# Two transformer blocks on one core: the first product behind each norm takes x times the gain, and 1/rms is applied to what leaves PSUM

## The reference, cut to what matters

```python
def first_block(x, mem, ...):
    for l in range(DEPTH):                                                     # DEPTH = 2
        x = x + FFN_RES_WEIGHT * swiglu_ffn(rms_norm(x, ffn1_norm_g[l]), ...)    # n = 0
        proj = rms_norm(x, mix_norm_g[l]) @ w_mix_in[l]                         # n = 1
        ...                                                # RWKV time mix, local attention
        x = x + jnp.concatenate([y_rwkv, y_moba], axis=-1) @ w_mix_out[l]
        x = x + memory_cross_attention(rms_norm(x, xattn_norm_g[l]), ...)       # n = 2
        x = x + FFN_RES_WEIGHT * swiglu_ffn(rms_norm(x, ffn2_norm_g[l]), ...)    # n = 3
    return rms_norm(x, final_norm_g)
```

## Time and profile before

| | us |
|---|---|
| median of 3 runs (lowest to highest) | 2770.87 (2770.12 to 2775.54) |
| the profiled execution's own time | 2772.01 |
| its span in the trace | 2770.0 |
| PE busy in the span | 2631.0 |
| DVE busy | 1680.3 |
| ACT busy | 1020.7 |
| mean granted TensorE clock | 0.973 of full speed |

### The profile page before, as it was taken

The page is one execution under the profiler, slowest core; times in us unless marked ns, Lnnn a source line. Parts: engine busy times, 40 slices in busy tenths (PEclk is TensorE's granted clock), DMA queues, the critical chain, the costliest instruction groups (busy, mean ns, idle before and its releaser), DMA issues. The chain is left out here.

```text
span 2770.0 us, 44598 instructions
## 1 busy us (share of the span) xinstructions
PE 2631.0 (95%) x18787; PEld 2325.1 (84%) x18787; DVE 1680.3 (61%) x2235; ACT 1020.7 (37%) x1241; POOL 99.2 (4%) x179
## 2 busy tenths in 40 slices
PE   8999989889999999989979999999999999989999
PEld 8999888879989999888879974355699899737999
DVE  6877655657777777656648742364455555354555
ACT  4335303434333345204443322453333333254333
POOL 2110000000100100000001100000000000000000
PEclk9999989999999999999999999999999999999999
DMA  8776201535767775003527772100355555210452
GB/s 274 258 258 195 80 1 47 190 130 184 259 229 233 259 241 168 31 1 109 196 91 235 260 259 77 61 16 16 122 183 182 196 184 183 93 61 31 137 183 92
DMA packets 279509, 415.62 MB, mean 150 GB/s; under 512 B 10105, under 2 KB 235721, under 8 KB 277698
## 3 DMA queue, kind: packets, MB, share of 16 engines
q1 hardware_dynamic: 260332, 348.16, 38.1%
q0 software_dynamic: 18128, 64.20, 6.6%
q10 hardware_dynamic: 902, 1.15, 0.1%
HBM read 399.82 MB, written 13.65 MB: 149 GB/s over the span
## 5 line engine op out<-in xcount | busy, mean ns | idle before, releaser
L572 PE MATMUL ps<-h_high,w_high 128*128 128x256 f32 x2112 | 609.1, 288 | 27.5 <-DVE h_low L1305 15.0
L574 PE MATMUL ps<-h_high,w_low 128*128 128x256 f32 x2144 | 613.0, 286 | 0.0
L572 PEld LDWEIGHTS ps<-h_high,w_high 128*128 128x128 f32 x2112 | 412.7, 195 | 32.8 <-issue 29.3
L574 PEld LDWEIGHTS ps<-h_high,w_low 128*128 128x128 f32 x2144 | 418.3, 195 | 0.0
L573 PE MATMUL ps<-h_low,w_high 128*128 128x256 f32 x1408 | 401.4, 285 | 0.0
L1320 DVE TENSOR_TENSOR w_low<-ring,w_high 128x2048 fp32r<-128x2048 f32 x132 | 301.9, 2289 | 132.7 <-ACT w_high L1080 132.6
L2659 DVE TENSOR_TENSOR w_low<-ring,w_high 128x2048 fp32r<-128x2048 f32 x96 | 220.0, 2292 | 240.7 <-ACT w_high L2443 240.5
L1080 ACT ACTIVATE w_high<-ring 128x2048 fp32r<-128x2048 f32 x132 | 251.6, 1914 | 267.8 <-DMA ring<-in_ffn_w_in 150.6
L2443 ACT ACTIVATE w_high<-ring 128x2048 fp32r<-128x2048 f32 x96 | 183.8, 1916 | 331.4 <-PE ps L2122 304.3
L573 PEld LDWEIGHTS ps<-h_low,w_high 128*128 128x128 f32 x1408 | 273.6, 194 | 0.0
L1341 DVE SCALAR_TENSOR_TENSOR mod_acc<-wmod,cond,mod_acc 128x512 f32<-128x512 f32 x336 | 230.5, 746 | 0.0
(11 more groups left out here) (411 smaller groups left out, 5168.1 us busy)
## 6 DMA issues: line engine op xcount, KB each, us to landing
ring<-in_w_mlp SPq DMA_DIRECT2D x96, 1024.0 KB, 5.4
ring<-in_ffn_w_in SPq DMA_DIRECT2D x88, 1024.0 KB, 8.3
wmod<-in_w_mod POOLq DMA_DIRECT2D x96, 512.0 KB, 6.3
ring<-in_ffn_w_out SPq DMA_DIRECT2D x44, 1024.0 KB, 5.1
ring<-in_w_mix_in SPq DMA_DIRECT2D x26, 1024.0 KB, 5.5
ring<-in_xattn_w_kv SPq DMA_DIRECT2D x16, 1024.0 KB, 5.4
mod_scratch<-mod_acc POOLq DMA_DIRECT2D x24, 512.0 KB, 5.4
ring<-mod_scratch SPq DMA_DIRECT2D x12, 1024.0 KB, 6.9
```

Source lines behind the costliest of these rows:

```text
L572: mm(dst, w_hi, x_hi, start=start, stop=False, **more)
L574: return mm(dst, w_lo, x_hi, start=False, stop=stop, **more)
```

## The change

For the seven norms other than the very first, ACT writes `high` straight from x times the gain as soon as a pair of x is final (`gained_high`), and DVE the rest (`gained_low`). The first product behind the norm runs on these, without 1/rms; what leaves PSUM is multiplied by 1/rms (`by_root`), now by DVE: in the FFN the first gate and up products (before and beside the SiLU), in the mix its first tile, in the cross attention all four `xq` tiles (which ACT evacuated before). For n = 2 the normed operand is no longer made at all; for the others it is made as before and the second product waits for it. The sums move between the pairs of the first product. On ACT the squares of norm 3 move ahead of the weight tiles, and two table preloads go. The copies of `mem` move ahead of layer 0's mix norm on DVE.

```diff
 # PE
+        def gained_pair(l, n, p):
+            pe.wait_ge(*g_low_ready.at(*gained_at(l, n, 2 * p + 1)))
...
             def first_gate_up():
                 halves = [parts(r, 0, r, r) for r in range(2)]
+                if f:
+                    pe.wait_ge(*x_ready.at(l, 4 * 2 + 3))
                 for p in range(KD // 2):
-                    pe.wait_ge(*h_ready.at(l, H_READY[3 * f] + SPLIT_AT[p]))
-                    for r, bank in ((0, 4), (1, 6)):
+                    for q in (((), (3,), (), ()) if f else ((), (1, 2), (3,), ()))[p]:
+                        sums(l, 3 * f, q)
+                    gained_pair(l, 3 * f, p)
+                    for r, bank in ((0, 5), (1, 6)):
...
-                for q in range(1, 4):
-                    if then:
-                        sums(*then, q)
...
-            gate_up(1, 1, 2, 2, False)
+            gate_up(1, 1, 2, 2, False, normed(l, 3 * f) if l or f else None)
...
+                if n == 0:
+                    def first_pair(p):
+                        for q in ((), (1, 2), (3,), ())[p]:
+                            sums(l, 1, q)
+                        gained_pair(l, 1, p)
+                    column_tile(l, ("mix_in", j), mix_bank(0), g_high, g_low, before=first_pair)
...
-            sums(l, 2, 3)
+            def xq_pair(p):
+                if p == 2:
+                    sums(l, 2, 3)
+                gained_pair(l, 2, p)
             for j in range(LIN_TILES):
-                column_tile(l, ("xq", j), 4 + j % 4, h_high, late_low, before=None if j else normed(l, 2))
+                column_tile(l, ("xq", j), xq_bank(j), h_high, late_low, before=None if j else xq_pair)
...
 # ACT
+        def gained_high(l, n, q):
+
+            high, _ = gained(n)
+            for k in (2 * q, 2 * q + 1):
+                go(high[:, k, :], x_sb[:, k, :], ACT.Copy, scale=gain_of(l, n, k)).then_inc(*g_high_ready.up())
...
-            if n == 3:
-                col_high(l, XO0 + 3, XO0 + 1)
-            if n == 3 or (n == 0 and l):
-                first_high(l, n // 3)
+            if n == 0 and l:
+                first_high(l, 0)
...
-            nc.scalar.preload_act_table_set(LN_EXP)
+            if n < 2:
+                nc.scalar.preload_act_table_set(LN_EXP)
...
+                if n or l:
+                    gained_high(l, n, q)
+                if n == 2 and q == 2:
+                    col_high(l, XQ0 + 1)
+                if n == 3 and q == 0:
+                    w_high_part(FfnTiles(l, 1), 0, 0, 0, 0)
+                    col_high(l, XO0 + 3, XO0 + 1)
+                if n == 3 and q == 1:
+                    w_high_part(FfnTiles(l, 1), 1, 0, 0, 1)
...
 # DVE
+        def gained_low(l, n, q):
+
+            high, low = gained(n)
+            for k in (2 * q, 2 * q + 1):
+                dve.wait_ge(*g_high_ready.at(*gained_at(l, n, k)))
+                v.scalar_tensor_tensor(low[:, k, :], x_sb[:, k, :], gain_of(l, n, k), high[:, k, :],
+                                       ALU.mult, ALU.subtract).then_inc(*g_low_ready.up())
...
             w_low_of(0, 1, 2, 2)
-            times_up(0, 0, 0, False)
+            if l or f:
+                dve.wait_ge(*std_ready.at(l, 6 * f + 2))
+                for r, dst, bank in ((0, prob, 5), (1, act_whole, 6)):
+                    dve.wait_ge(*tiles.used(r, 0, 0))
+                    v.tensor_tensor(dst[:, 0, :].rearrange("p (m t) -> p m t", m=2),
+                                    ps[bank].rearrange("p (m t) -> p m t", m=2), by_root(), ALU.mult
+                                    ).then_inc(*first_scaled.up())
...
-            dve.wait_ge(*mix_evac.at(l, n + 1))
             b = raw[:, n % 2]
+            if n:
+                dve.wait_ge(*mix_evac.at(l, n))
+            else:
+                dve.wait_ge(*column_used(l, MIX_ORDER[0]))
+                dve.wait_ge(*std_ready.at(l, 4))
+                step(l, v.memset(raw[:, :, :, 0:1], 0.0), mixed)
+                step(l, v.tensor_tensor(b[:, :, 1:T + 1], ps[mix_bank(0)].rearrange("p (m t) -> p m t", m=2),
+                                        by_root(), ALU.mult), raw_evac)
...
-            norm(l, 2, "xattn_norm_g")
+            col_low(l, XQ0 + 1)
             col_low(l, XQ0 + 2)
-            modulate(l, 0, second, range(0, 4))
+            dve.wait_ge(*std_ready.at(l, 6))
+            modulate(l, 0, second, range(0, 2))
+            xq_scaled(l, 0)
+            modulate(l, 0, second, range(2, 4))
+            xq_scaled(l, 1)
             col_low(l, XQ0 + 3)
             col_low(l, XO0)
+            xq_scaled(l, 2)
             modulate(l, 0, second, range(4, 6))
             col_low(l, XO0 + 1)
+            xq_scaled(l, 3)
             softmax(l, XH, NH, XD ** -0.5, (T, T), cross_out(l))
```

More of the change, by code:

```diff
@@ L300, in build_first @@
         late_low = part("late_low", [P, KD, T])
+        part("under_mem", [P, KD, T])
+        part("under_hank", [P, NH, T])
+        g_low = part("g_low", [P, KD, T])
+        part("under_low", [P, RAW + 4 * T - KD * T])
+        g_high = part("g_high", [P, KD, T])
         w_high.append(h_low[:, :, :].rearrange("p k t -> p (k t)"))
@@ L612, in first_gate_up, with gate_up @@
                             last.then_inc(w_used[tiles.slot(r, 0)].sem, 1)
-            def gate_up(i, b, t, buffer, reuse):
-                for r, bank in ((0, 4 + b), (1, 6 + b)):
+            def gate_up(i, b, t, buffer, reuse, before=None):
+                for r, bank in ((0, 5 - b), (1, 6 + b)):
                     hi, lo = parts(r, b, t + r, (buffer + r) % W_HIGHS)
@@ L621, in gate_up @@
                         for k in range(KD):
+                            if before and r == 0 and m == 0 and k % 2 == 0:
+                                before(k // 2)
                             cols = slice(m * P, (m + 1) * P)
@@ L1286, in residual, with first_low, one_behind, after @@
                     after(q)
[L1288 to L1289 removed]
+        def first_low(l, f, rs=(0, 1)):
+            for r in rs:
                 w_low_part(FfnTiles(l, f), r, 0, r, r)
+        def gained_low(l, n, q):
[4 more added lines that the diff above has]
+                                       ALU.mult, ALU.subtract).then_inc(*g_low_ready.up())
+        def one_behind(l, n):
+            def after(q):
+                for p in ((), (0,), (1,), (2, 3))[q]:
+                    gained_low(l, n, p)
+            return after
         def col_low(l, c):
@@ L1396, in ffn @@
                 col_low(l, 1)
-            residual(l, 3 * f, [None] * 3 + [tiles.n0 + FFN_TILES - 1], 0.5)
+            residual(l, 3 * f, [None] * 3 + [tiles.n0 + FFN_TILES - 1], 0.5,
+                     None if f and l + 1 == DEPTH else one_behind(l + f, 1 - f))
         def step(l, instruction, signal=None):
@@ L1555, in recurrence, with mix_out_after, xq_scaled, xo_after @@
                                         ALU.mult), seq_step)
+        def mix_out_after(l, q):
+            if q < 3:
+                col_low(l, MIX_OUT0 + 2 + q)
+            gained_low(l, 2, q)
+        def xq_scaled(l, j):
+            n = FIRST_AT[("xq", j)]
+            dve.wait_ge(w_used[n % RING].sem, freed(n, l) + 1)
+            v.tensor_tensor(xq[:, 2 * j:2 * j + 2, :], ps[xq_bank(j)].rearrange("p (m t) -> p m t", m=2),
+                            by_root(), ALU.mult).then_inc(*xq_evac.up())
+        def xo_after(l, q):
+            gained_low(l, 3, q)
+            if q == 0:
+                first_low(l, 1, (0,))
+                col_low(l, XO0 + 3)
+            if q == 1:
+                first_low(l, 1, (1,))
         w_low_part(FfnTiles(0, 0), 0, 0, 0, 0)
@@ L1580, in vector_program @@
                 v.tensor_copy(bias_rows, ps[1][0:NH, :]).then_inc(*mem_placed.up())
-            step(l, v.memset(raw_buf[:, :], 0.0), mixed)
+            norm(l, 1, "mix_norm_g")
             for n, j in enumerate(MIX_ORDER[:7]):
@@ L1674, in vector_program @@
             modulate(l, 0, second, range(6, KD))
-            residual(l, 2, [FIRST_AT[("xo", j)] for j in range(LIN_TILES)], 1.0,
-                     lambda q: col_low(l, XO0 + 3) if q == 1 else first_low(l, 1) if q == 2 else None)
+            residual(l, 2, [FIRST_AT[("xo", j)] for j in range(LIN_TILES)], 1.0, lambda q: xo_after(l, q))
             norm(l, 3, "ffn2_norm_g")
```

133 lines of the change are left out of this document (84 added, 49 removed).

## The result

| | before | after |
|---|---|---|
| median of the runs taken together | 2773.2 us (4 runs) | 2742.25 us (2741.4 to 2746.6, 4 runs) |
| profiled execution: time, span | 2772.01, 2770.0 | 2742.86, 2740.9 |
| mean granted clock | 0.973 | 0.973 |

After over before is 0.9892, with a 95% interval of [0.9875, 0.9909]: about 1.1% faster, by 31.0 us between the medians and 25 to 35 us by the interval. The forecast was 2728 with a range up to 2741, and the median lies 1.25 us outside it. The gain forecast was 42.6.

The account below looks back on a forecast made before the run. PE was taken as the bound, busy 95%, with about 47 of 139 idle us at the seven norms. Terms 14.6 + 13.9 + 7.4 + 6.3 + 3.4 - 2.4 - 0.6 = 42.6 us gave a 2728.3 us median, range 2717 to 2741.

Parts of the forecast that it names:

- The second block and the FFN steps past the second are the same.: Claim that the second block and FFN steps beyond the second keep their time; no gain or loss counted there.
- half rate after the short new waits: Rival: new waits of 0.6 to 2.1 us halve the clock, 1.9 us at six places, 11.4; 2740 us, chance 0.15.
- only the 6.1 us wait pays: Reading of the skill page: clock falls only behind the wait at step 1's gate tile, layer 1's FFN 1; 1.9 us.
- FFN 2, layers 0, 1: Norm 3 and FFN 2: earlier squares and first products on the gained operand; 14.6 and 13.9 us gained.
- `xq`, layers 0, 1: Norm 2 and xq product: it starts right after the sums, so cross attention comes 7.4 and 6.3 us earlier.
- mix, layers 1, 0: Norm 1 and the mix's first tiles: 3.4 us gained in layer 1, 0.6 us lost in layer 0.
- norm 0 of layer 1: Layer 1's first FFN: step 0 starts earlier, but step 1's gate tile waits 6.1 us; 2.4 us lost.
- the walk: Each engine's operation list timed part by part from unit prices; 38 to 47 us gained, chance 0.53, forecast 2728.
- The prices: Assumed unit times: gain multiplication 0.49 us, `gained_low` 0.4 to 0.48, multiplying a bank by 1/rms 0.69.
- At nothing: ACT's gain multiplications (3.9 us a norm) and DVE's `gained_low` (3.4) lie hidden under PE's work, costing nothing.
- The slower rival: Rival: without norm gaps the weight DMA falls behind in three FFNs; at 1.5 us a step, 2778 us, chance 0.03.
- the signs named beforehand: Trace signs: right, about 2 us before cross attention; wrong, mix clock at 0.50 or waits at step 1's up tile.

Follow-up runs that it names:

- e9: Kernel before, one added DVE reduction lengthening PE's wait at the entry of the second block's first attention; 2790.99 us, ratio 1.0062.
- e10: Changed kernel, extra matmuls filling only the third wait, at the entry of the second block's attention, in both layers; 2731.83 us, ratio 0.9855.
- e11: Changed kernel unaltered, timed again in one job; 2732.89, 2733.31, 2743.57 and 2744.32 us.
- e1: Changed kernel, extra matmuls filling PE's three last waits before the second block's attention, in both layers; 2731.54 us, ratio 0.9844.
- e4: Changed kernel, 16 extra matmuls ahead of the second block's first product; 2751.12 us, one run.
- e7: Changed kernel, 4 extra matmuls ahead of the second block's first product, same program as e2, timed in rounds; 2735.93 to 2751.48 us, median 2747.24.
- e3: Changed kernel, 8 extra matmuls ahead of the second block's first product; 2736.88 us, one run.
- e5: Kernel before with only ACT's order at norm 3 changed (first squares ahead of weight halves, no table preload there); 2756.63 us, ratio 0.9952.
- e8: Kernel before with extra matmuls filling the three waits before the second block's attention; 2772.27 us, ratio 1.0001.
- e2: Changed kernel, 4 extra matmuls ahead of the second block's first product; 2726.17 us, one run.
- e6: Changed kernel with the three waits filled as in e1 and step 1's weight halves made ahead of the norm; 2716.82 us, ratio 0.9810.

## Why the prediction was wrong

**The step that failed** is "The second block and the FFN steps past the second are the same." Its instructions and waits are; its clock is not. In the two profiled executions the second block, from the first key rotation to the first output product, went from 117.9 to 137.3 us: 19.4 lost, after 4.6 gained ahead of it (6.3 us of clock lost there before, 1.6 after). With 42.8 at its start and 1.1 behind it that makes the 29.1 of the spans. e9 and e10 show the cause from both sides. I had priced a fall of the clock by the matmuls that follow it in the first block, where I took 1.9 to 3 us each; none of my cases had one that lasts. The trace of before had them all the same: in layer 0's time mix, among products of 64 and 128 columns, its windows from 384 to 396 are at 0.50, one of them (388 to 392) with PE busy 4.00 of 4.00. Where the changed kernel is spared, it ran at 2732.9 and 2733.3 (e11), inside the range, though 5 us above the forecast of 2728.

**The rival "half rate after the short new waits"** gave 2740, near the median, and that is luck. Its mechanism is there at two of its places. In the changed kernel's own trace the clock falls 1 us behind layer 1's wait of 1.84 us (1408.59), for 3.4 us:

```profile
1408.00:1410.00 2.00, 1.41 (x10) 0.90 1.08 369
1410.00:1412.00 2.00, 2.00 (x11) 0.50 0.91 280
1412.00:1414.00 2.00, 2.00 (x15) 0.75 0.64 224
```

All eight traces with the changed first block (after, e1 to e4, e7, e10, e11) have this fall, and three of them (e1, e3, e11) one like it behind layer 0's wait at 618 to 620; in the changed kernel's trace the matmuls behind that wait (617.97) take 0.28 to 0.38 us, at 1.00. Each costs 1.7 us of clock. Behind the other new waits, 0.60 and 0.91 in the mix (1014.13 and 1021.02 in layer 1) and 1.43 before cross attention, no trace has one. So the rival is worth 1.7 to 3.4 us, and the 19.4 us are lost elsewhere: it looked for the fall only at the waits that the change makes. Its sum is wrong as well: it lists eight places (two in each mix, one in each cross attention, one in each FFN 2) and multiplies by six; eight times 1.9 is 15.2, 2743.5, past the end of the range. By the page "TensorE: Matmul & The Clock Gate" of the Trainium skill (HAM oscillation), as the prediction cites it, only the 6.1 us wait pays; the falls behind waits of 1.82 to 1.84 us say otherwise, and the measurement decides.

**The terms of the sum**, in us gained:

| term | forecast | measured in the two traces |
|---|---|---|
| FFN 2, layers 0, 1 | 14.6, 13.9 | 14.6, 13.8 |
| `xq`, layers 0, 1 | 7.4, 6.3 | 8.1, 7.1 |
| mix, layers 1, 0 | +3.4, -0.6 | +3.2, -0.4 |
| norm 0 of layer 1 | -2.4 | -3.9 |
| between these places | 0 | +0.3 |
| first block | 42.6 | 42.8 |

The waits forecast at 1.8 us in each FFN 2 and at 6.1 in layer 1's FFN 1 measured 1.84 and 6.01; e5 agrees with the split between ACT's order and the gained operand. `xq` gained 0.7 and 0.8 more because the wait before cross attention is 1.43 and not 2.1. The term of norm 0 was the one mis-sized, by 1.5. There the clock falls behind the wait of 3.26 us, as before, but what runs slowly now is more than I had counted: the sums end 1.8 us later in the frame of before than the 832.4 of the walk. So the gate tile starts 2.2 us behind the kernel before, where the walk had 0.5; the clock behind it costs 1.7 (forecast 1.9). The fall behind layer 1's gate tile in FFN 2 is in no term. It does not show in the 42.8 because the kernel before lost as much to a fall at 1632, behind a wait of 1.92 us, that the changed kernel's trace does not have. The +0.3 is itself a sum of parts up to 1.7 us: in layer 0's time mix and local attention the changed kernel's trace gained 1.7, in layer 1's it lost 0.7.

**How sure that sum is.** One pair of traces agrees to 0.2 us by luck. Over the eight traces with the changed first block its end lies between 1627.0 and 1632.3 (mean 1629.5), over the six with the old one between 1670.9 and 1675.4 (mean 1672.7): the difference of the means is 43.2. Most of the spread is the clock's: up to that point it lost 39.3 us in one trace with the changed first block (e10) and 48.2 in another (e11).

**The prices** held: `gained_high` 0.495 us (forecast 0.49), `gained_low` 0.483 (0.4 to 0.48), the scaled bank 0.686 (0.69). "At nothing" held too: no wait of PE for a gained half. The slower rival did not come: PE has no wait for a weight DMA in the FFN steps. Of the signs named beforehand the right ones came (the wait before cross attention shorter than the "about 2"), and none of the wrong ones: no window below 1.00 at the norm of the mix, no wait for step 1's up tile. None of the signs looked at the second block.

## What to carry to other kernels

Take a gain as two sums: the time that the walk gives where the code changes, and the clock in every stage behind it, also where not an instruction changed. Look there for waits of 1 to 2 us just ahead of a long run of short matmuls, as this attention of 256- and 128-column products; a fall there can cost ten times the wait (in this attention it did, in that of the second layer never), and in only some executions, so compare several profiles of one kernel before a difference is put down to an edit. Such a wait can be filled with a few matmuls into a bank that is overwritten anyway, measured for their real length; where there was no long stretch the fill gained nothing (e8). And when an operand is made early, make the weights of the product behind it early as well, or the wait only moves.

## What the hardware showed that I had not expected

- Once at half rate at the entry of this attention, PE stayed there for about 40 us, though its windows are busy 4.00 of 4.00 (after, e4, e7; e9 with the longer wait). Elsewhere in these traces the longest stretch is 17 us, in the first block's time mix. That it is no fault of the record is seen from the matmuls started, 12 to 15 in 4 us against 19 to 25. The page "TensorE: Matmul & The Clock Gate" of the Trainium skill (Seeing it yourself) warns that the clock has been seen stuck at a quarter for more than 50 us and that its trace events are not always to be trusted; the runs here show a shorter stretch, and at half.
- Waits of 1.82 to 1.84 us took the clock down for 3.4 us at 11 of 16 places (FFN 2 in eight traces), always in layer 1 and in three traces in layer 0.
- One program gives different clocks: e2 and e7 (2726.2, and 2735.9 to 2751.5). In every trace 51 to 94 us in sum are lost to windows below full clock, except in e6 (43).
- The clock also falls where PE is never idle: in the kernel before at 1738.6, with 1.00 us of 1.00 busy in the windows ahead of it and behind it.
- A float32 matmul of 256 columns leaves two records and costs about 0.43 us; one of the split halves costs 0.12.
